# Modulation product in column strips, output pieces turned one per turn, half tiles of a V projection paired

## The chip, the cores and the metric

The kernel runs on one core of one Trainium2 chip. The metric is the device time of one execution, in microseconds; lower is better. TensorE (PE) multiplies, VectorE (DVE), ScalarE (ACT) and GpSimd (POOL) do the rest, and the sync engine (SP) issues most transfers.

## What is computed

Two blocks on 512 tokens of width 1024, all in float32. The first is an RWKV-7 time mixer with 16 heads of 64, whose recurrence is worked out in chunks of 64 tokens. The second is a block with a Fourier branch and a neighbourhood attention over the tokens and 256 context tokens; both inputs are normed and then modulated by a shift and a scale. The part of the reference that the change touches, cut to what matters (the bodies of the helpers are left out):

```
sh_x, sc_x, g_x = modulation of silu(c) @ w_ada + b_ada        # (1024) @ (1024, 3072)
sh_c, sc_c, g_c = the same for c_ctx
xn = rms_norm(x) * (1 + sc_x) + sh_x
cn = rms_norm(ctx) * (1 + sc_c) + sh_c
... vx ... = xn @ w_in        ... vc ... = cn @ w_in
y = (groupnorm(y) + bonus * v) * g                             # end of the RWKV mixer
out = y @ w_out
```

## The kernel before

One program of five instruction streams, one per engine, written out by hand and tied by semaphores; each engine works strictly in the order of its own stream. Weights come in 74 blocks through a ring of three buffers (`weights`, L469): SP may load block n when the engine that uses block n-3 is done with it.

The recurrence is a loop of 21 turns, g = -1 to 19 (L787 for PE, L1275 for ACT, L1631 for DVE). There are 16 groups of work (8 chunks by 2 halves of the heads). In turn g, PE starts group g+1 (`off_product` L656, `turned` L639, `grow` L668 and L670), goes on with group g (`rhs_values` L681, with `gram` L624 for group g+2) and finishes group g-1 (`from_state` L698 and L705, `scan_sa` L716, `scan_out` L729 and L737). Between them ACT and DVE take results out of PSUM: `mask_gram` L1564, `mask_z` L1572, `add_x` L1581, `update` L1595 and L1596 on DVE; `copy_sa` L1252, `copy_y` L1258 on ACT. At the end of some turns DVE also norms a finished quarter of y: `centre` (L1605 to L1607) where g % 4 is 1, a sum of squares (L1655) where it is 2, a scaling (L1658, L1659) where it is 3.

Two other pieces of work stand inside the turns. **Modulation**: silu(c) and silu(c_ctx), as two columns `SILC`, times `w_ada`, in 12 blocks of 256 output columns. `mods_here(g, k)` (L774) puts a block into slot k of turn g by the table `MODS_BY` (L457): slot 0 lies between `turned` and `grow`, slot 1 between `rhs_values` and `gram`. A slot is `turn_mods` (L755, two small transposes of the block before, copied to `MROW` by ACT, L1264) and `modulation` (L741, eight products through `accumulate` L513, with the two columns stationary and 128x256 weights moving). Before, turns 0 to 5 carry two blocks each, and turn 6 the last `turn_mods`. DVE then makes shift and scale of them (`take_mods`, L1618) at the end of turn 7. **Turning**: in turns 8, 12 and 16, PE turns a quarter of y in four pieces of four transposes (`turn_y`, L759, L771): pieces 0 and 2 from y, 1 and 3 from the bonus values. All use bank 3, the bank of the modulation too, and so each waits until the piece before is taken: 0 and 2 by ACT (`take_y`, L1271), 1 and 3 by DVE (`finish_y`, L1614, L1616).

Later, in the second block, `vv` (L905) is the V projection: for two halves of 256 columns, seven tiles of 128 tokens (five of the padded tokens `XNP`, two of the context) each in eight products of `accumulate`, two tiles to a bank. `XNP` is 64 zero columns, 512 tokens and 64 zero columns wide, so the first half of tile 0 and the last half of tile 4 are zeros. ACT takes the banks (`take_v`, L1358). The K projection behind it (L507 to L509) uses weights that ACT and DVE split into two parts (L1118, L1706).

A product of plain float32 shows as two instructions in the trace; a transpose as one.

## Time and profile before

| what | value |
|---|---|
| median of 3 runs | 916.29 us (915.19 to 919.98) |
| the profiled execution | 915.69 us, of it 913.9 us span |
| mean granted clock | 0.942 |
| TensorE busy | 809.0 us, 89% |
| VectorE, ScalarE, GpSimd busy | 501.6, 301.0, 209.4 us |
| bytes moved | 72.82 MB, 80 GB/s |

The span runs from the first to the last instruction; the time of the execution holds 1.8 us more. A wait in square brackets at the end of a row is idle time of that engine just before the instruction, with the instruction that ended it. In the view by stretch a row has the stretch, its length, then busy time and number of instructions of PE, PE's weight loads, DVE, ACT and POOL, then granted clock, share of the DMA engines and GB/s. A granted clock of 1.00 is 2.4 GHz, of 0.50 is 1.2 GHz; a share between is a stretch that had both.

### The profile page before, as it was taken

To read this page: it belongs to the slowest core of one execution; us is meant where nothing else is said; L and a number is where in the kernel's file an instruction comes from. 1 tells how busy PE (TensorE), PEld (TensorE's weight loads), DVE (VectorE), ACT (ScalarE), POOL (GpSimd) and SP (SyncE) were. 2 spreads that over 40 slices of the span, in tenths; PEclk is the share of its full clock that TensorE was granted. 3 is DMA by queue.
4 is the path that set the end of the run, shared out by engine and by line. 5 is a ranking of instruction groups with operands and counts; after the bars stand their busy time and mean duration, and the time that the engine had idled before them with its cause. 6 is when DMAs were issued, how large, how long until landed. Compare 5 with 4: busy or idle time off the path is not lost.

```text
span 913.9 us, 17380 instructions
## 1 busy us (share of the span) xinstructions
PE 809.0 (89%) x7476; PEld 642.2 (70%) x7476; DVE 501.6 (55%) x799; ACT 301.0 (33%) x625; POOL 209.4 (23%) x162
## 2 busy tenths in 40 slices
PE   2599998999796899987877899999979988989997
PEld 2288775777585566676876788888756766767597
DVE  4973998988676212165544212802995646543711
ACT  6334433455331112132323135512334433322410
POOL 0254422445343011132211000630000000000662
PEclk9799999999798799998988999999998998989999
DMA  7023241323437544410003033401320211121221
GB/s 219 23 74 108 73 136 48 93 70 82 103 116 185 117 140 140 141 48 3 4 3 139 30 109 91 87 24 47 93 69 24 59 37 45 47 81 47 93 82 58
DMA packets 116621, 72.82 MB, mean 80 GB/s; under 512 B 26816, under 2 KB 113984, under 8 KB 116544
## 3 DMA queue, kind: packets, MB, share of 16 engines
q1 hardware_dynamic: 81856, 64.07, 23.3%
q10 hardware_dynamic: 34688, 7.62, 4.1%
q8 instruction: 60, 0.98, 0.4%
q14 instruction: 17, 0.14, 0.0%
HBM read 64.35 MB, written 7.34 MB: 78 GB/s over the span
## 4 chain that ended last, share of the span: by engine, by line
PE 76%; DVE 13%; ACT 3%; issue 2%; DMA 2%; ACTq 1%; POOL 1%; POOLq 0%; DVEq 0%
PE bank L513 24%; PE bank L932 8%; PE bank L507 5%; PE bank L508 5%; PE bank L509 5%; DVE arena L1466 3%; PE bank L954 2%; PE bank L967 2%; PE bank L624 2%; DVE arena L1564 2%; PE bank L670 2%; PE bank L656 2%; PE bank L1050 1%; PE bank L1052 1%; PE bank L1051 1%
## 5 line engine op out<-in xcount | busy, mean ns | idle before, releaser
L513 PE MATMUL bank<-arena 128*128 128x256 f32 (+2 forms) x1024 | 242.3, 396 | 4.5 <-DVE arena L1616 3.1
L513 PEld LDWEIGHTS bank<-arena 128*128 128x128 f32 (+1 forms) x1024 | 175.9, 175 | 62.9 <-issue 17.3
L1869 POOL TENSOR_TENSOR w_lo<-arena,w_hi 128x1024 fp32r<-128x1024 f32 x24 | 62.6, 2610 | 110.6 <-ACT w_hi L1118 110.6
L507 PE MATMUL bank<-x_hi,w_hi 128*128 128x512 f32 x192 | 80.5, 419 | 4.9 <-DVE x_lo L1472 4.9
L1118 ACT ACTIVATE w_hi<-arena 128x1024 fp32r<-128x1024 f32 x44 | 46.5, 1057 | 93.6 <-DMA arena<-w_in 92.3
L509 PE MATMUL bank<-x_hi,w_lo 128*128 128x512 f32 x192 | 77.1, 402 | 0.0
L508 PE MATMUL bank<-x_lo,w_hi 128*128 128x512 f32 x192 | 77.0, 401 | 0.0
L1971 POOL COPY arena<-arena 128x512 f32<-128x512 f32 x4 | 2.5, 614 | 223.8 <-DVE arena L1789 223.8
L507 PEld LDWEIGHTS bank<-x_hi,w_hi 128*128 128x128 f32 x192 | 37.1, 193 | 15.8 <-issue 7.7
L1564 DVE TENSOR_TENSOR arena<-bank,arena 128x512 f32<-128x512 f32 x32 | 20.6, 686 | 49.0 <-PE bank L624 49.0
L1706 DVE TENSOR_TENSOR w_lo<-arena,w_hi 128x1024 fp32r<-128x1024 f32 x20 | 25.0, 1250 | 38.3 <-ACT w_hi L1118 38.3
L1908 POOL TENSOR_TENSOR arena<-arena 128x512 f32<-128x512 f32 x16 | 20.1, 1258 | 110.0 <-PE bank L716 106.7
L1768 DVE TENSOR_REDUCE arena<-bank 128x1 f32<-128x256 f32 x32 | 13.6, 424 | 56.4 <-PE bank L947 56.4
L508 PEld LDWEIGHTS bank<-x_lo,w_hi 128*128 128x128 f32 x192 | 37.2, 194 | 9.9 <-issue 1.7
L509 PEld LDWEIGHTS bank<-x_hi,w_lo 128*128 128x128 f32 x192 | 37.1, 193 | 8.7
L932 PE MATMUL bank<-xn_hi,w_hi 128*128 128x512 f32 x96 | 41.3, 430 | 0.0
L1466 DVE SCALAR_TENSOR_TENSOR arena<-arena 128x512 f32<-128x512 f32 x48 | 40.6, 916 | 0.0
L1581 DVE TENSOR_TENSOR arena<-arena,bank 128x128 f32<-128x128 f32 x48 | 12.0, 285 | 51.5 <-PE bank L670 51.4
L932 PE MATMUL bank<-xn_lo,w_hi 128*128 128x512 f32 x96 | 39.1, 407 | 0.0
L932 PE MATMUL bank<-xn_hi,w_lo 128*128 128x512 f32 x96 | 38.8, 404 | 0.0
L1404 ACT ACTIVATE arena<-arena 128x256 f32<-128x256 f32 x32 | 16.3, 509 | 62.2 <-DVE arena L1772 61.6
L1050 PE MATMUL bank<-w_out_hi,mix_hi 128*128 128x256 f32 x128 | 36.5, 286 | 0.2 <-DVE mix_lo L1836 0.2
(237 smaller groups left out, 1691.9 us busy)
## 6 DMA issues: line engine op xcount, KB each, us to landing
arena<-w_in SPq DMA_DIRECT2D x45, 512.0 KB, 4.0
arena<-w_ada SPq DMA_DIRECT2D x12, 1024.0 KB, 5.2
arena<-w_in SPq DMA_DIRECT2D x8, 1024.0 KB, 5.6
arena<-w_out SPq DMA_DIRECT2D x8, 1024.0 KB, 5.1
lt_dram<-arena ACTq DMA_DIRECT2D x16, 256.0 KB, 2.3
arena<-x SPq DMA_DIRECT2D x4, 512.0 KB, 7.3
arena<-x SPq DMA_DIRECT2D x1, 2048.0 KB, 7.7
out<-arena SPq DMA_DIRECT2D x8, 256.0 KB, 2.6
```

The costliest lines, as they stand in the source:

```text
L507: mm(o[:, :], w_hi[:, wk], x_hi, start=(k == 0), stop=False)
L508: mm(o[:, :], w_hi[:, wk], x_lo, start=False, stop=False)
L509: return mm(o[:, :], w_lo[:, wk], x_hi, start=False, stop=(k == KT - 1))
L513: last = mm(o, lhs(k), rhs(k), start=(k == 0), stop=(k == n - 1))
L932: last = mm(banks[5 + i % 2][:, :], w[slot][:, k * P:(k + 1) * P], v[k][:, :], start=(r == 0), stop=(r == 3 * KT - 1))
L1050: mm(oi, MXHI[k][:, at], W2HI[nb][:, wk], start=(k == 4), stop=False)
L1118: A(WHI[n % 3][:, :], WR[n % 3][:, 0:1024], ACT.Copy).then_inc(weights_rounded, 1)
L1466: ins = STT(MIXES[m][:, c, :], DX[:, c, :], vec("mu_" + "wakrvg"[m], c), HT[:, c, 1:T + 1], MUL, ADD)
L1564: free(TT(GM[g % 4][:, h], o, gram_mask.unsqueeze(1).broadcast_to([P, 4, 2 * CH]), MUL), ("gram", g, h))
L1706: TT(WLO[n % 3][:, :], WR[n % 3][:, 0:1024], WHI[n % 3][:, :].bitcast(f32), SUB)\
L1869: TT(WLO[n % 3][:, :], WR[n % 3][:, 0:1024], WHI[n % 3][:, :].bitcast(f32), SUB)\
L1908: TT(XS[:, g % 3].rearrange("p s c (m n) -> p (s c) m n", n=BLK), x.unsqueeze(2).broadcast_to([P, 8, CH // BLK, BLK]), blocks.broadcast_to ...
```

## The change

Modulation: `SILC` is now 32 columns wide (two and thirty zeros, cleared by DVE). The eight products of a block go to four strips of 32 columns of the array, two products summed in each, and leave four partial sums in PSUM partitions 0, 32, 64 and 96. ACT copies all 128 partitions, and `turn_mods` is now two plain products with a constant `pick` (128x2, ones where the partition modulo 32 is the column), which turn and add the four in one. The last four blocks move to slot 1 of turns 4 to 7, the last `turn_mods` to turn 8 (slot 0), `take_mods` to the end of turn 8.

Turning: quarters 0 and 1 of y are turned one piece a turn, in turns 8 to 15; ACT takes its piece in the even turns, DVE in the odd ones. Quarter 2 still goes in one turn, 16.

V projection: tiles are taken in the order 1, 2, 3, 5, 6, 0. The last stands for tiles 0 and 4: their halves with tokens go side by side to two strips of 64 columns. The zero halves of V are cleared by GpSimd instead.

```diff
-               ("reset", T), ("dft128", 2 * P), ("eps", 3)]:
+               ("reset", T), ("dft128", 2 * P), ("eps", 3), ("pick", 2)]:
...
+    put("pick", (i % 32 == j[:, 0:2]).astype(f))
...
-        MROW = fixed.take(256, 2)
+        SILC = fixed.take(KT * 32).rearrange("p (c k) -> p c k", k=32)
...
+        MROW = arena[:, ht_at + 1536:ht_at + 1792]
...
+        V_TILES = (1, 2, 3, 5, 6, 0)
...
-        for n, (g, k) in enumerate([(0, 0), (0, 1), (1, 0), (1, 1), (2, 0), (2, 1), (3, 0), (3, 1), (4, 0), (4, 1), (5, 0), (5, 1),
-                                    (6, 1)]):
+        for n, (g, k) in enumerate([(0, 0), (0, 1), (1, 0), (1, 1), (2, 0), (2, 1), (3, 0), (3, 1), (4, 1), (5, 1), (6, 1), (7, 1),
+                                    (8, 0)]):
...
-                last = accumulate(banks[MODS_BANK][0:2, 0:256], lambda k: SILC[:, k, :], lambda k: w[:, k, :])
+                for r in range(2):
+                    for q in range(4):
+                        k = 2 * q + r
+                        last = mm(banks[MODS_BANK][32 * q:32 * q + 32, 0:256], SILC[:, k, :], w[:, k, :], start=(r == 0),
+                                  stop=(r == 1), skip_group_check=True)
...
-                    last = nc.tensor.transpose(banks[MODS_BANK][:, at:at + 2], MROW[:, h * P:(h + 1) * P], ident[0:2, 0:2])
+                    last = mm(banks[MODS_BANK][:, at:at + 2], MROW[:, h * P:(h + 1) * P], con("pick"), start=True, stop=True,
+                              skip_group_check=True)
...
-                if turning:
+                if 8 <= g < 16:
+                    turn_y(g // 4 - 2, g % 4)
+                if g == 16:
                     for piece in range(4):
-                        turn_y(g // 4 - 2, piece)
+                        turn_y(2, piece)
...
+                    for i, t in enumerate(V_TILES[2 * b3:2 * b3 + 2]):
+                        oi = o[:, i * 256:(i + 1) * 256]
+                        if t:
...
+                        for k in range(KT):
+                            for h, at in ((0, 4 * P), (1, HD)):
+                                last = mm(oi[side[h], :], XNP[:, k, at:at + HD], w[:, k, :], start=(k == 0),
+                                          stop=(k == KT - 1), skip_group_check=True)
...
-                    A(MROW, banks[MODS_BANK][0:2, 0:256], ACT.Copy).then_inc(mods_copied, 1)
+                    A(MROW, banks[MODS_BANK][:, 0:256], ACT.Copy).then_inc(mods_copied, 1)
...
-                if turning:
-                    take_y(g // 4 - 2, 0)
-                    take_y(g // 4 - 2, 1)
+                if 8 <= g < 16 and g % 2 == 0:
+                    take_y(g // 4 - 2, g % 4 // 2)
...
-                if turning:
-                    finish_y(g // 4 - 2, 0)
-                    finish_y(g // 4 - 2, 1)
+                if g == 8:
+                    take_mods()
+                if 8 <= g < 16 and g % 2 == 1:
+                    finish_y(g // 4 - 2, g % 4 // 2)
...
-                if g == 7:
-                    take_mods()
...
+            own.did(nc.gpsimd.memset(VP[:, 0:5:4, :], 0.0))
```

PE, a turn that lost its slot 0 and kept slot 1 (turn 4), from `off_product` of turn 4 on. The rows give line, operation, tiles, size and number. Before:

```order
L656 MATMUL bank<-arena 64x32 x16
L639 MATMUL bank<-arena 64x64 x16
L755 MATMUL bank<-arena 128x2 x2
L513 MATMUL bank<-arena 2x256 x8
L668 MATMUL bank<-arena 64x32
```

and now, where L658, L641, L670 stand for the old L656, L639, L668:

```order
L658 MATMUL bank<-arena 64x32 x16
L641 MATMUL bank<-arena 64x64 x16
L670 MATMUL bank<-arena 64x32
L672 MATMUL bank<-arena 64x32
L670 MATMUL bank<-arena 64x32
```

The table took slot 0 out of the turn: `grow` follows `turned` at once.

PE, end of turn 8 and start of turn 9. Before:

```order
L729 MATMUL bank<-arena 64x64 x8
L737 MATMUL bank<-arena 64x64 x8
L771 MATMUL bank<-arena 128x2x64 x16
L656 MATMUL bank<-arena 64x32 x16
L698 MATMUL bank<-arena 64x64 x8
```

and now:

```order
L731 MATMUL bank<-arena 64x64 x8
L739 MATMUL bank<-arena 64x64 x8
L778 MATMUL bank<-arena 128x2x64 x4
L658 MATMUL bank<-arena 64x32 x16
L700 MATMUL bank<-arena 64x64 x8
```

One piece of four transposes is left in the turn; the same four rows end each of turns 8 to 15.

DVE, from the end of turn 13 to the first `mask_z` of turn 14. Before:

```order
L1595 TENSOR_TENSOR arena<-bank,arena 128x256
L1596 TENSOR_TENSOR arena<-arena 128x256
L1605 TENSOR_REDUCE arena<-arena 128x16
L1606 TENSOR_SCALAR arena<-arena 128x16
L1607 TENSOR_TENSOR arena<-arena 128x1024
L1572 TENSOR_TENSOR arena<-bank,arena 128x8x16
```

and now:

```order
L1616 TENSOR_TENSOR arena<-bank,arena 128x256
L1617 TENSOR_TENSOR arena<-arena 128x256
L1635 TENSOR_TENSOR arena<-arena,bank 128x512
L1637 SCALAR_TENSOR_TENSOR arena<-arena 128x512
L1626 TENSOR_REDUCE arena<-arena 128x16
L1627 TENSOR_SCALAR arena<-arena 128x16
L1628 TENSOR_TENSOR arena<-arena 128x1024
L1593 TENSOR_TENSOR arena<-bank,arena 128x8x16
```

The two instructions of `finish_y` now stand ahead of `centre` and of the `mask_z` that PE waits for. The same pair stands at the end of turns 9, 11 and 15.

## Rows read from the trace of the kernel before

**Rows 1.** The page, part 1: busy time, share of the span and instructions of each engine.
```profile
PE 809.0 (89%) x7476; PEld 642.2 (70%) x7476; DVE 501.6 (55%) x799; ACT 301.0 (33%) x625; POOL 209.4 (23%) x162
```

**Rows 2.** The page, part 4: shares of the chain that ended last, by engine.
```profile
PE 76%; DVE 13%; ACT 3%; issue 2%; DMA 2%; ACTq 1%; POOL 1%; POOLq 0%; DVEq 0%
```

**Rows 3.** Busy time by stretch: turn 5, then turns 8 to 13 of the recurrence.
```profile
374.90:389.75 14.85, 14.33 (x277) 9.35 (x277) 2.96 (x9) 2.93 (x8) 2.04 (x3) 1.00 0.44 143
...
407.97:422.23 14.26, 9.67 (x256) 8.25 (x256) 7.27 (x18) 5.18 (x14) 2.44 (x4) 0.90 0.01 2
422.23:430.88 8.65, 8.15 (x242) 7.87 (x241) 4.17 (x10) 2.18 (x6) 1.66 (x2) 0.76 0.02 4
430.88:441.04 10.16, 8.27 (x241) 7.69 (x241) 6.29 (x13) 3.01 (x7) 3.78 (x4) 0.83 0.02 4
441.04:447.96 6.92, 6.42 (x240) 6.14 (x241) 4.46 (x11) 2.35 (x7) 2.54 (x4) 1.00 0.02 5
447.96:461.76 13.80, 9.75 (x258) 8.34 (x260) 6.81 (x15) 5.19 (x14) 2.45 (x4) 0.95 0.01 2
461.76:471.01 9.25, 8.75 (x240) 8.47 (x241) 4.19 (x10) 2.18 (x6) 1.66 (x2) 0.70 0.01 4
```

**Rows 4.** TensorE in order of time, slot 0 of turn 1; then one form's busy us, mean ns.
```profile
318.60 0.28 PE L755 MATMUL bank<-arena 2*128 2x2 f32 x2
318.81 3.61 PE L513 MATMUL bank<-arena 128*2 128x256 f32 x16
322.35 0.31 PE L668 MATMUL bank<-arena 64*64 64x32 f32 x4
322.49 0.29 PE L670 MATMUL bank<-arena 64*64 64x32 f32 x4
...
L513 PE MATMUL bank<-arena 128*2 128x256 f32 x192 | 44.9, 388 | 0.0
```

**Rows 5.** TensorE in order of time: products in half tiles; then L967's durations, ns min/median/max.
```profile
358.12 1.10 PE L624 MATMUL bank<-arena 64*64 64x128 f32 x32
...
747.07 1.09 PE L967 MATMUL bank<-arena 128*64 128x128 f32 x16
...
L967 PE MATMUL bank<-arena x256: 272/273/476, 703.5 to 830.3; 128*64 128x128 f32 x128
```

**Rows 6.** TensorE in order of time: pieces 0, 1 and 3 turned in turn 8.
```profile
415.18 0.66 PE L771 MATMUL bank<-arena 128*128 128x128 f32 x4
417.43 0.65 PE L771 MATMUL bank<-arena 128*128 128x128 f32 x4 [1.59 <-ACT arena L1271]
...
421.19 1.11 PE L771 MATMUL bank<-arena 128*128 128x128 f32 x4 [1.59 <-ACT arena L1271]
```

**Rows 7.** VectorE in order of time, end of turn 8.
```profile
415.86 0.60 DVE L1596 TENSOR_TENSOR arena<-arena 128x256 f32<-128x256 f32 x1
418.19 0.69 DVE L1614 TENSOR_TENSOR arena<-arena,bank 128x512 f32<-128x512 f32 x1 [1.74 <-PE bank L771]
418.92 0.69 DVE L1616 SCALAR_TENSOR_TENSOR arena<-arena 128x512 f32<-128x512 f32 x1
```

**Rows 8.** TensorE in order of time: the wait for `mask_z` in turns 8 and 10.
```profile
410.89 0.31 PE L668 MATMUL bank<-arena 64*64 64x32 f32 x4 [0.55 <-DVE arena L1572]
...
434.89 0.31 PE L668 MATMUL bank<-arena 64*64 64x32 f32 x4 [1.64 <-DVE arena L1572]
```

**Rows 9.** TensorE in order of time: second V projection, what follows it.
```profile
578.70 48.51 PE L513 MATMUL bank<-arena 128*128 128x256 f32 x224
626.86 0.58 PE L507 MATMUL bank<-xn_hi,w_hi 128*128 128x512 f32 x1
```

**Rows 10.** VectorE and GpSimd in order of time, around the second V projection.
```profile
591.98 1.87 DVE L1706 TENSOR_TENSOR w_lo<-arena,w_hi 128x1024 fp32r<-128x1024 f32 x1
...
562.17 0.85 POOL L1947 MEMSET arena<- 128x256 f32 x1
```

**Rows 11.** The page, part 6: a transfer of modulation weights.
```profile
arena<-w_ada SPq DMA_DIRECT2D x12, 1024.0 KB, 5.2
```

More of the change, by code:

```diff
@@ L182, in rwkv_then_grid_block @@
         GST = small(64 * 3)
-        SILC = small(16).rearrange("p (c k) -> p c k", k=2)
         SILT = small(32)
@@ L788, in _ @@
                 now, nxt, old = 0 <= g < GROUPS, g + 1 < GROUPS, 0 < g <= GROUPS
-                turning = g in (8, 12, 16)
                 if nxt:
@@ L906, in _ @@
                 w = weights()
-                for b4 in range(4):
-                    o = next_bank(("vv", nb, b4))
-                    for i in range(2):
-                        t = 2 * b4 + i
-                        if t < 7:
-                            last = accumulate(o[:, i * 256:(i + 1) * 256],
-                                              (lambda k: XNP[:, k, t * P:(t + 1) * P]) if t < 5 else
-                                              (lambda k: CNT[:, k, (t - 5) * P:(t - 4) * P]), lambda k: w[:, k, :])
-                    full(last, ("vv", nb, b4))
+                for b3 in range(3):
+                    o = next_bank(("vv", nb, b3))
+                    for i, t in enumerate(V_TILES[2 * b3:2 * b3 + 2]):
+                        oi = o[:, i * 256:(i + 1) * 256]
+                        if t:
+                            last = accumulate(oi, (lambda k: XNP[:, k, t * P:(t + 1) * P]) if t < 5 else
+                                              (lambda k: CNT[:, k, (t - 5) * P:(t - 4) * P]), lambda k: w[:, k, :])
+                            continue
+                        for k in range(KT):
+                            for h, at in ((0, 4 * P), (1, HD)):
+                                last = mm(oi[side[h], :], XNP[:, k, at:at + HD], w[:, k, :], start=(k == 0),
+                                          stop=(k == KT - 1), skip_group_check=True)
+                    full(last, ("vv", nb, b3))
             for name in ("kk", "q"):
@@ L981, in _ @@
             for nb in range(2):
-                for b4 in range(4):
-                    stored(pe, ("vv", nb, b4))
+                for b3 in range(3):
+                    stored(pe, ("vv", nb, b3))
             for p in range(PU + 2):
@@ L1276, in _ @@
                 nxt, old = g + 1 < GROUPS, 0 < g <= GROUPS
-                turning = g in (8, 12, 16)
                 if old:
@@ L1290, in _ @@
                     fetch_inverse(1)
-                if turning:
-                    take_y(g // 4 - 2, 0)
-                    take_y(g // 4 - 2, 1)
+                if 8 <= g < 16 and g % 2 == 0:
+                    take_y(g // 4 - 2, g % 4 // 2)
+                if g == 16:
+                    take_y(2, 0)
+                    take_y(2, 1)
                 j = g // 4 - 1
@@ L1354, in take_v @@
                 for nb in range(2):
-                    for b4 in range(4):
-                        o = arrived(act, ("vv", nb, b4)).rearrange("p (i n) -> p i n", i=2)
-                        w = 2 if b4 < 3 else 1
-                        free(A(VP[:, 2 * b4:2 * b4 + w, nb * 256:(nb + 1) * 256], o[:, 0:w, :], ACT.Copy), ("vv", nb, b4))
+                    at = slice(nb * 256, (nb + 1) * 256)
+                    for b3 in range(3):
+                        o = arrived(act, ("vv", nb, b3)).rearrange("p (i n) -> p i n", i=2)
+                        if b3 < 2:
+                            t = V_TILES[2 * b3]
+                            ins = A(VP[:, t:V_TILES[2 * b3 + 1] + 1:b3 + 1, at], o, ACT.Copy)
+                        else:
+                            A(VP[:, 6, at], o[:, 0, :], ACT.Copy)
+                            for h, t in ((0, 4), (1, 0)):
+                                ins = A(VP[side[h], t, at], o[side[h], 1, :], ACT.Copy)
+                        free(ins, ("vv", nb, b3))
             def round_xn():
@@ L1445, in _ @@
             own.did(nc.vector.memset(CST, 0.0))
+            own.did(nc.vector.memset(SILC, 0.0))
             own.did(nc.vector.memset(HT[:, :, 0:1], 0.0))
@@ L1456, in _ @@
             own.own(TS(SILT[:, 16:32], SILT[:, 0:16], 0.5, 0.5, MUL, ADD))
-            own.did(TT(SILC.rearrange("p c k -> p k c"), SILT[:, 16:32].rearrange("p (k c) -> p k c", k=2),
+            own.did(TT(SILC[:, :, 0:2].rearrange("p c k -> p k c"), SILT[:, 16:32].rearrange("p (k c) -> p k c", k=2),
                        VECS[:, VEC["c"]:VEC["c"] + 16].rearrange("p (k c) -> p k c", k=2), MUL))
@@ L1632, in _ @@
                 now, nxt, old = 0 <= g < GROUPS, g + 1 < GROUPS, 0 < g <= GROUPS
-                turning = g in (8, 12, 16)
                 if nxt:
@@ L1646, in _ @@
                     update(g - 1)
-                if turning:
-                    finish_y(g // 4 - 2, 0)
-                    finish_y(g // 4 - 2, 1)
+                if g == 8:
+                    take_mods()
+                if 8 <= g < 16 and g % 2 == 1:
+                    finish_y(g // 4 - 2, g % 4 // 2)
+                if g == 16:
+                    finish_y(2, 0)
+                    finish_y(2, 1)
                 j = g // 4 - 1
```

## Prediction

> **What bounds the kernel now.** I read the page first. TensorE is busy 89% of the span [rows 1], and 76% of the chain that ended last is its work [rows 2]. So instructions taken off TensorE shorten the kernel, unless something else then ends the same turn. The busy time by stretch shows this for the recurrence, one row per turn [rows 3]. A turn without extras takes 6.92 us, of it 6.42 busy (turn 11). A turn with two modulation slots takes 14.85 (turn 5). A turn that turns four pieces takes 14.26 or 13.80 (turns 8 and 12), with 9.7 busy: the rest is waiting. The turns behind these, 9 and 13, take 8.65 and 9.25 at a clock of 0.76 and 0.70, so the waits cost a second time. Turn 10 follows `centre` and takes 10.16, at 0.83.
>
> **The modulation blocks.** In a slot the 16 instructions start every 0.215 us (3.61 less the last one's own 0.38, over 15), and from the block's start to `grow` it is 3.54 us [rows 4]. Each is 256 columns wide, so 0.215 us is the price of 256 columns on the full array, whether 2 or 128 stationary columns are used. What do strips give? Nothing in the trace has four strips. The nearest rows are products in halves [rows 5]. L967, two strips of 64 columns under all 128 rows, does 16 instructions of 128 columns in 1.09 us, one alone 0.27: 0.82 over the seven steps between eight pairs, about 0.11 to 0.12 a pair. That is about the full-array price of one (0.215 / 2), so two strips run fully side by side. L624 has four quarter tiles: 32 instructions of 128 columns in 1.10 us, seven steps in 0.83 after the first four, so four run side by side. Those are the two bounds: four strips fourfold, 16 x 0.215 / 4 = 0.86 us a block, or only twofold, 1.72. I add 0.10 for the change of shape, the 3.54 less 16 x 0.215. I take fourfold, since L624 is the row with four tiles. 12 x (3.54 - 0.96) = **31.0 us off**, all on the path, as no slot is preceded by a wait. The Trainium skill, TensorE: Matmul & The Clock Gate, section on packing small matmuls, gives a measured 2.38x for three column strips. At that efficiency, an estimate from that page, a block takes 1.09 and the sum is 2.7 us worse; the trace shows two strips at no loss, and no run here four.
>
> `turn_mods` becomes two float32 products, four instructions with 128 stationary columns each. Before, the next block starts 0.21 us after it starts [rows 4]. Four transposes with 128 stationary columns take 0.66 [rows 6], one alone 0.27 as in rows 5, so 0.13 a step. At 0.11 (half of 0.215) to 0.13 each that is about 0.44 a time: 12 x 0.23 = **2.8 us back**.
>
> Moving two slots out of turns 4 and 5 and into 6 and 7 changes no count. The weights stay ahead: one block's transfer takes 5.2 us [rows 11], three are in flight, and a turn of two blocks will take some 10 us. Even one after the other, block 7 lands about 30 us into the loop and is needed at about 36. Cost nothing; if that cover went, 1 or 2 us.
>
> **The turning.** In turn 8, PE waits 1.59 us before pieces 1 and 3 until ACT has taken the one before [rows 6], and less before piece 2. With one piece a turn these go. A single piece (0.5 to 0.6) mostly lies in the 0.50 that PE idles in each plain turn (6.92 less 6.42 [rows 3]), which is the wait for `mask_gram` at its start, so I cost it at 0.1 while that cover is there, 0.55 in turns 14 and 15, where there is no such wait. But two things are added.
> - In turn 8 the first piece needs bank 3, which `take_mods` frees. `take_mods` now stands behind `update`, which ends at 416.46 [rows 7], while PE's piece was ready at 415.18 [rows 6]. With `turn_mods` 0.4 later and 0.2 for the read, PE waits some 1.6 us. Against that the wait for `mask_z` in turn 8, 0.55 [rows 8], to which `take_mods` at the end of turn 7 belonged, goes. The next turn then starts near 417.2 instead of 422.23: **5.0 off**.
> - `finish_y` takes 1.42 us on DVE, from 418.19 to 419.61 [rows 7]. It now stands ahead of `centre` or the scaling in turns 9, 11, 13 and 15. Queued behind it are the `mask_z` that PE's `grow` waits for. Turn 10 already waits 1.64 there [rows 8]; it becomes 3.06. Turn 12 had none; it gets 1.4. Turn 14 is like turn 10.
>
> Turn by turn: turn 9 back to plain, 8.65 - 6.92 = 1.7 off. Turn 10, 1.4 on. Turn 12, 13.80 - 6.92 = 6.9 off, 1.4 on. Turn 13, 9.25 - 6.92 = 2.3 off. Turn 14, 1.9 on with its piece. Turns 15 and 16, 1.3 on (the piece, and some of `finish_y`, which now delays the third quarter). For the clock I add what turn 10 lost beyond its wait, 10.16 - 6.92 - 1.64 = 1.6, once more, because longer waits will let it fall again somewhere. With turn 8: -5.0 - 1.7 + 1.4 - 5.5 - 2.3 + 1.9 + 1.3 + 1.6 = **8.3 off**.
>
> **The V projection.** 224 instructions in 48.5 us, 0.215 each, and the K projection follows without a wait [rows 9]. Per half, 32 of 112 instructions (tiles 0 and 4) become 32 of half width. By L967 a pair of them costs what one full instruction costs: 16 x 0.215 = 3.44 instead of 6.88. Twice 3.44 = **6.9 us off**. The cover of what runs beside it holds: the split weights for the K projection are done at 593.85 [rows 10], the new end is near 620. GpSimd's added clearing is 1,024 wide, four times its 256-wide one of 0.85 [rows 10]: 3.4 us behind 563.0 at most, with the V projection starting at 578.70: nothing. The wider `SILC` clearing and ACT's extra copies lie under waits for transfers.
>
> **The sum.** 31.0 - 2.8 + 8.3 + 6.9 = 43.4 us. Against the profiled execution, 915.7, that is **872.3 us**. This execution lies 0.6 us below the median of 916.3; I leave that alone.
>
> **The rivals.**
> - Strips overlap only twofold. The two instructions of one product share a strip; if the engine starts matmuls strictly in program order, the second holds back the next strip, and only neighbours overlap. For it: no row has four strips. Against: L668 and L670 alternate in the program, yet run four and four [rows 4], and L624 runs four tiles at once [rows 5]. Price: 12 x 0.86 = 10.3 us, so 882.6. The Trainium skill, same page and section, says that matmuls are "strict FIFO, no reordering"; by that rule, this would be the outcome.
> - DVE becomes the bound of the late turns. If turns 10, 12 and 14 each lose the 1.6 us of clock on top of their longer waits, and turn 8 also, three more of them add 4.8; with pieces not hidden under the 0.50, eight times 0.5 more: 881. For it: turn 10's clock fell after 1.64 us of waiting [rows 3, 8]. Against: only DVE's order, not its load, is tight, 4.46 of 6.92 in turn 11.
> - Slower than before: four strips of 32 columns don't overlap, and each instruction waits for the one before to end, 0.38 instead of 0.215 [rows 4]. Place: the 12 blocks. A block then takes 6.06 + 0.10 us, 12 x 2.62 = 31.4 on. With the other terms, 12.4 off, that is 915.7 + 31.4 - 12.4 = 934.7. It decides from 4.6 us a block. Against it: halves do overlap [rows 5], and strips of 32 are a finer cut of the same thing. If they run one after the other without a gap, a block costs what it did and the time is 903.
>
> **Chances.** Forecast (872) 0.68; twofold 0.16; DVE and clock 0.09; no overlap, no gap 0.03; slower 0.03; something else, still faster, 0.01. The range for 8 in 10 must hold the forecast with its own spread, from -7 (no clock falls after the waits, and the wait at bank 3 is hidden) to +6, and the two rivals near 882: **865 to 885**. A measurement of this kernel tells about 0.5%, 4.6 us, from no change. Faster by more than that 0.96, within it 0.01, slower 0.03.
>
> **What would show it.** Blocks of 32-column products of about 0.95 us, or 1.8 (twofold), or over 4.6. Turns 1 to 3 of 9.4 to 10.2 us. No wait of 1.59 for ACT in turns 8 to 15, one of about 1.6 for DVE at bank 3 in turn 8, and waits for `mask_z` of about 3 us in turns 10 and 14, 1.4 in turn 12. The V projection at 41.6 us with no wait behind it. The prediction is wrong if a block lasts over 1.3 us, or if the turns from 8 to 15 are not some 8 us shorter in all.

## The result, and the profile after

The change takes the kernel from 916.22 us (median of 4 runs, 915.19 to 919.98) to 889.80 us (median of 4 runs: 892.07, 887.52, 896.19, 887.32). The ratio is 0.9708, 95% interval 0.9665 to 0.975. So 26 us are gone where the prediction had 43, and the time lies outside the predicted range of 865 to 885. The order of the four times is the order of their mean granted clocks: 0.934 twice (887), 0.925 (892), 0.920 (896); runs of before, taken beside the experiments below, spread as widely, from 914 us at 0.942 to 923 at 0.932. The profiled execution is the one of 892.07 us, with a span of 890.3, so one of the two slower.

The page, part 1, of the changed kernel, for [rows 1]:

```profile
PE 787.9 (89%) x7500; PEld 636.6 (72%) x7500; DVE 502.8 (56%) x800; ACT 301.5 (34%) x627; POOL 210.4 (24%) x163
```

TensorE is busy for 21.1 us less than before, and its share is the same 89%. Part 4, for [rows 2], where "issue", time in which an engine waited for nothing visible, has gone from 2% to 3%:

```profile
PE 76%; DVE 14%; issue 3%; ACT 3%; DMA 2%; ACTq 1%; POOL 1%; POOLq 0%; DVEq 0%
```

**The strips themselves did what was forecast.** TensorE in order of time, turn 2, for [rows 4]: start and length in us, line, form, count.

```profile
336.92 0.61 PE L761 MATMUL bank<-arena 128*128 128x2 f32 x4
337.45 1.07 PE L751 MATMUL bank<-arena 128*32 128x256 f32 x16
338.45 1.10 PE L626 MATMUL bank<-arena 64*64 64x128 f32 x32
```

From the block's start to the next work it is 1.00 us (337.45 to 338.45), forecast 0.96, where it was 3.54. In the trace the sixteen start in four groups of four, 0.007 us apart within a group and 0.22 to 0.24 us from group to group. `turn_mods` takes 0.53 (336.92 to 337.45), forecast 0.44. The V projection, for [rows 9]:

```profile
561.62 17.43 PE L515 MATMUL bank<-arena 128*128 128x256 f32 x80
578.98 3.67 PE L925 MATMUL bank<-arena 128*64 128x256 f32 x32
...
603.65 0.50 PE L509 MATMUL bank<-xn_hi,w_hi 128*128 128x512 f32 x1
```

It lasts 42.03 us, 6.1 less than before, and nothing waits behind it.

**The turns did not follow.** Busy time by stretch, one row a turn, turns 0 to 15 (5, 7, 9, 11 and 13 left out; they take 9.35, 9.43, 7.83, 7.54 and 6.99): the stretch, its length, busy us of PE, PEld, DVE, ACT, POOL, then the granted clock, the DMA share and GB/s.

```profile
300.05:314.29 14.24, 12.64 (x196) 9.48 (x197) 2.65 (x7) 1.70 (x5) 0.00 (x0) 0.50 0.56 144
314.29:330.60 16.31, 16.31 (x249) 13.04 (x249) 2.64 (x7) 2.57 (x7) 1.25 (x1) 0.50 0.43 137
330.60:341.15 10.55, 10.04 (x282) 8.42 (x281) 3.30 (x9) 2.95 (x8) 2.45 (x4) 0.98 0.52 158
341.15:352.43 11.28, 9.90 (x281) 8.29 (x281) 4.20 (x11) 3.23 (x9) 2.44 (x4) 1.00 0.68 216
352.43:361.28 8.85, 7.73 (x229) 6.70 (x229) 2.88 (x8) 2.18 (x6) 1.66 (x2) 1.00 0.29 87
...
370.63:384.26 13.63, 11.48 (x260) 9.65 (x261) 6.36 (x13) 3.94 (x9) 4.00 (x4) 0.75 0.28 94
...
393.69:404.87 11.18, 9.52 (x249) 8.72 (x249) 5.80 (x16) 2.18 (x6) 2.70 (x4) 0.85 0.17 61
...
412.70:425.00 12.30, 8.82 (x245) 8.27 (x244) 8.20 (x15) 3.02 (x7) 4.00 (x4) 0.86 0.02 3
...
432.54:441.11 8.57, 7.25 (x246) 6.70 (x245) 6.05 (x14) 2.19 (x6) 2.06 (x3) 1.00 0.02 4
...
448.10:461.11 13.01, 9.15 (x214) 8.54 (x213) 7.16 (x14) 3.02 (x7) 2.76 (x4) 0.74 0.01 3
461.11:469.46 8.35, 6.42 (x182) 5.57 (x182) 4.71 (x8) 4.26 (x12) 0.58 (x1) 1.00 0.01 2
```

Look at the clock of the first two rows, and then at the same two turns of before:

```profile
300.89:317.05 16.16, 14.56 (x194) 8.34 (x195) 2.62 (x7) 1.67 (x5) 0.00 (x0) 0.82 0.44 104
317.05:331.13 14.08, 13.57 (x244) 8.58 (x245) 2.87 (x8) 2.55 (x7) 1.66 (x2) 1.00 0.48 154
```

The forecast had 9.4 us less in turns 0 and 1, and they take the same time: 30.5 us for 30.2. The clock comes down to its lower level (0.50, 1.2 GHz) in the wait ahead of the recurrence in both kernels. Before, it was back at the upper one (1.00, 2.4 GHz) at 306.9:

```profile
289.80:306.90 17.10, 12.56 (x208) 9.43 (x201) 3.94 (x9) 1.32 (x4) 5.29 (x7) 0.50 0.50 70
306.90:331.10 24.20, 22.12 (x367) 13.28 (x365) 4.88 (x13) 3.56 (x10) 1.66 (x2) 1.00 0.47 148
```

Now it is not back before 331.0:

```profile
290.00:331.00 41.00, 35.51 (x581) 28.34 (x574) 8.93 (x22) 4.93 (x14) 6.79 (x9) 0.50 0.51 131
```

The other large item is the waits in the late turns. TensorE's waits from turn 0 on, by line and what ended them: us in total, times, longest.

```profile
PE bank L670 <- DVE arena L1593: 9.9, 4, 3.5
PE bank L658 <- DVE arena L1585: 5.8, 7, 1.6
...
PE bank L672 <- issue: 1.7, 3, 0.8
PE bank L658 <- issue: 1.4, 1, 1.4
PE bank L778 <- DVE arena L1643: 1.2, 1, 1.2
PE bank L718 <- issue: 1.2, 2, 0.6
```

The first row is `mask_z` at 3.48 in turns 10 and 14, 1.63 in turn 6 and 1.32 in turn 12, for [rows 8]. The three rows with "issue" make 4.3 us, with 0.5 of L670 4.8, in seven waits; before there was one, of 0.59, in turn 7.

Set against the prediction's own terms, by groups of turns (us, profiled executions):

| turns | before | forecast | after | missed by |
|---|---|---|---|---|
| 0, 1 (four blocks) | 30.2 | 20.9 | 30.5 | 9.6 |
| 2 to 5 (eight blocks, now six) | 58.6 | 37.0 | 40.0 | 3.0 |
| 6, 7 (none, now two) | 18.2 | 20.8 | 23.1 | 2.3 |
| 8 to 15 (the turning) | 79.6 | 71.7 | 75.8 | 4.1 |
| V projection | 48.2 | 41.3 | 42.0 | 0.7 |

The last column makes 19.7 of the 19.8 us between 872.3 and 892.07.

### The profile page after: what moved, and what is told of

Same layout as the page of the kernel before. It is cut to its first block, busy times and chain, and to the rows that moved or that the text cites. A ratio compares the mean times of both kernels' runs of the same rounds, so it can differ in the third digit from the quotient of the medians.

```text
span 890.3 us, 17431 instructions
## 1 busy us (share of the span) xinstructions
PE 787.9 (89%) x7500; PEld 636.6 (72%) x7500; DVE 502.8 (56%) x800; ACT 301.5 (34%) x627; POOL 210.4 (24%) x163
## 3 DMA queue, kind: packets, MB, share of 16 engines
q1 hardware_dynamic: 81856, 64.07, 23.9%
## 4 chain that ended last, share of the span: by engine, by line
PE 76%; DVE 14%; issue 3%; ACT 3%; DMA 2%; ACTq 1%; POOL 1%; POOLq 0%; DVEq 0%
PE bank L515 18%; PE bank L944 8%; PE bank L509 5%; PE bank L510 5%; PE bank L511 5%; DVE arena L1487 3%; PE bank L626 2%; PE bank L966 2%; PE bank L672 2%; PE bank L979 2%; PE bank L751 2%; PE bank L658 2%; DVE arena L1585 2%; PE bank L1062 1%; PE bank L1064 1%
## 5 line engine op out<-in xcount | busy, mean ns | idle before, releaser
L515 PE MATMUL bank<-arena 128*128 128x256 f32 (+1 forms) x768 | 184.3, 399 | 4.6 <-DVE arena L1637 3.1
L515 PEld LDWEIGHTS bank<-arena 128*128 128x128 f32 x768 | 148.2, 196 | 38.4 <-issue 15.4
L1424 ACT ACTIVATE arena<-arena 128x256 f32<-128x256 f32 x32 | 16.3, 510 | 61.8 <-DVE arena L1794 61.2
L1064 PE MATMUL bank<-w_out_hi,mix_lo 128*128 128x256 f32 x128 | 36.0, 282 | 0.0
```

The costliest lines, as they stand in the source:

```text
L515: last = mm(o, lhs(k), rhs(k), start=(k == 0), stop=(k == n - 1))
L1064: last = mm(oi, MXLO[k][:, at], W2HI[nb][:, wk], start=False, stop=(k == 3))
```

## The experiments

The theories. CLOCK: the dense blocks at the start had raised the clock, and the strips do the same work without raising it. WORK, its rival: the strips are worth less on the path than their own length says, whatever the clock. For the late turns, FINISH: the two instructions of `finish_y` ahead of the next `mask_z` are paid in full. All times are medians; each ratio is to the kernel before, run beside it (916 us each time).

**1. The old form of the blocks, the rest as changed (e1_full_blocks).**

```
-  for r in range(2): for q in range(4): last = mm(bank[32q:32q+32, 0:256], SILC[:, k, :], w[:, k, :], ...)
+  last = accumulate(bank[0:2, 0:256], lambda k: SILC[:, k, 0:2], lambda k: w[:, k, :])
```

(with the old copy of two rows and the old transposes).

> The changed kernel with the twelve modulation blocks and their turning back in the old form (two stationary columns, full array), all else as changed. The changed kernel took 889.8 us where 872.3 was forecast. Theory CLOCK: the strips are as fast as forecast, but TensorE's granted clock stays at 0.50 through turns 0 and 1 (290 to 331 us) because the dense blocks that raised it at 307 us are gone. Then here turns 1 and 2 run at 1.00 again, turn 1 takes about 14.1 us instead of 16.3, and the strips turn out to be worth only some 18 us: about 908 us. Rival WORK: the low clock there has nothing to do with the strips; it stays low here too until 331, and the kernel takes the full 28 us more, 918.

Measured: 906.73 us (904.5 to 908.79), ratio 0.989 (0.9857 to 0.9923). Its clock, to the end of turn 1:

```profile
289.70:306.70 17.00, 13.14 (x210) 9.59 (x202) 3.94 (x9) 1.32 (x4) 5.31 (x7) 0.50 0.50 73
306.70:330.66 23.96, 21.85 (x366) 13.19 (x365) 4.91 (x13) 3.56 (x10) 1.65 (x2) 1.00 0.47 149
```

Nothing but the dense blocks was put back, and the early rise is there again. The time is near CLOCK's 908 and not at WORK's 918. By the medians the strips are worth 16.9 us (906.73 less 889.80), not the 28.2 of the sum (31.0 less 2.8).

**2. Dense work ahead of turn 0 (e2_warm).** Seven products of 512 columns without a use, four behind the last g product and three behind `gram(0)`:

```
+            for _ in range(4):     # and range(3) behind gram(0)
+                mm(banks[6][:, :], ident, con("reset"), start=True, stop=True)
```

> The changed kernel with seven dense products of constants (128x128 by 128x512, into a bank nobody reads) put where TensorE only waits before the recurrence: four behind the last g product, three behind the first gram. Their result is used by nobody. Theory CLOCK: the clock no longer falls at 290 us, turns -1, 0 and 1 run at 1.00: about 2.5 us less in turn -1, 3 in turn 0, 7 in turn 1, together 10 to 12 us off: 879 us. If strips cannot hold the clock up by themselves, it falls again within turn 0 or 1 and only 3 to 5 us are won: 885. Rival WORK (clock not decisive there): no gain, 890, or 1 to 3 us slower by the added products.

Measured: 887.27 us (886.59 to 891.41), ratio 0.9688. The clock stayed up until 299.60, and then:

```profile
291.79:299.60 7.81, 6.22 (x184) 4.84 (x186) 2.70 (x8) 0.66 (x2) 5.22 (x7) 1.00 0.41 64
299.60:326.90 27.30, 25.70 (x378) 19.59 (x373) 4.71 (x12) 4.16 (x12) 1.25 (x1) 0.50 0.58 154
```

The 2.5 us by which the median is lower are within the noise (the intervals of the two ratios overlap); the trace is what counts here. It is not only that the recurrence begins at the lower level. In turns 0 and 1 with strips the clock falls by itself, though TensorE is busy for 25.70 of the 27.30 us.

**3. The turning as before (e3_no_spread).** All four pieces, with `take_y` and `finish_y`, at the end of turns 8 and 12 again; `take_mods` stays at the end of turn 8.

```
-                if 8 <= g < 16:
-                    turn_y(g // 4 - 2, g % 4)
+                if g in (8, 12, 16):
+                    for piece in range(4):
+                        turn_y(g // 4 - 2, piece)
```

> The changed kernel with the turning of y back in turns 8 and 12, four pieces in one turn; take_mods stays at the end of turn 8. The forecast for the spreading was 8.3 us off. If that holds, 898. The trace of the changed kernel shows for turns 8 to 15 waits of 3.5 us in turns 10 and 14 and clocks of 0.86 and 0.74; summed over turns 8 to 15 it took 75.8 us against 77.1 before, with one piece of turn_mods and the bank 3 wait in it. Theory DVE ORDER: the spreading is worth only 1 to 4 us, because finish_y now delays mask_z: 891 to 894. Rival: it is worth its 8, and the time was lost elsewhere.

Measured: 897.6 us (889.69 to 898.47), ratio 0.9763 (0.9707 to 0.9818). By the medians that is 7.8 us over the changed kernel, by the ratios 5.0, and the intervals overlap: whether the spreading gains anything is not settled by the time. Nor is this run the turning of before. With `take_mods` at the end of turn 8 its turn 8 takes longer than the 14.26 us of [rows 3], for TensorE waits 1.48 us for it at bank 3 and then for each piece:

```profile
389.21:406.03 16.82, 10.84 (x260) 9.16 (x260) 7.27 (x18) 5.20 (x14) 2.45 (x4) 0.89 0.12 42
```

Turns 8 to 14 take 78.2 us in this profile, 71.1 before and 67.4 in the changed kernel. So the run cannot confirm the 8.3 of the sum, which was reckoned from before. The 897.6 is the rival's 898, but the theory of VectorE's order isn't refuted by it: run 7 bears it out.

**4. The V projection as before (e4_no_pair).**

```
-  V_TILES pairs, tiles 4 and 0 as halves side by side in one piece of the bank
+  for b4 in range(4): for i in range(2): accumulate over whole tiles 0 to 6
```

> The changed kernel with the second V projection as before (seven full tiles, no pairing, no clearing of V by GpSimd). The trace shows 42.0 us for it where there were 48.2: 6 us slower, 896, if nothing behind it takes the gain back; 890 if something does.

Measured: 896.18 us (893.51 to 898.73), ratio 0.9775, 6.4 us over the change, forecast 6.9; the intervals of the two ratios just overlap. In its trace the projection is again 224 instructions, from 561.34 to 609.49 (48.15 us). This term held.

**5. One dense block (e7_dense_first).** Block 0, in slot 0 of turn 0, is one accumulation into rows 0 to 31; blocks 1 to 11 in strips.

```
+                if n < 1:
+                    last = accumulate(banks[MODS_BANK][0:32, 0:256], lambda k: SILC[:, k, :], lambda k: w[:, k, :])
```

> Against the change, only block 0 of the modulation product (turn 0) is put back into one dense accumulation of eight products (into rows 0 to 31 of the bank, the copy and the turning of that block over these rows); the other eleven stay in column strips. Theory CLOCK (the change lost what it had saved because in turns 0 and 1 the array was too little used for the clock to rise, 0.50 until 331.0 us where before it rose at 306.9): the dense block costs some 3 us more in turn 0 (5.1 for 1.9), the clock is up soon behind it, turn 1 lasts 10.4 to 11 us for 16.3 and the rest of turn 0 goes faster: 884 us, with one stretch at 0.50 that ends near 307. Rival RATE (it is not the first block but the dense work over both turns that raises the clock): the clock stays at 0.50 until about 331, turn 0 is 3 us longer: 893 us. Rival NOISE (the clock's phase decides, not the work): anything between, and no link to the first block.

Measured: 885.98 us (884.65 to 887.51), ratio 0.9662 (0.961 to 0.9714). Turns 0, 1 and 4:

```profile
299.81:314.09 14.28, 12.68 (x197) 8.50 (x197) 2.62 (x7) 1.69 (x5) 0.00 (x0) 0.77 0.50 116
314.09:323.74 9.65, 9.14 (x249) 7.52 (x249) 2.88 (x8) 2.57 (x7) 1.66 (x2) 1.00 0.71 225
345.67:357.62 11.95, 11.95 (x228) 10.10 (x229) 2.65 (x7) 2.18 (x6) 1.26 (x1) 0.57 0.29 91
```

The dense block takes 5.52 us in place of 1.93, most of it at the lower clock, and for that turn 1 takes 9.65 instead of 16.31: 6.6 us less for the two turns, as CLOCK has it. Half of it went again where the clock fell once more, in turn 4 (11.95 for 8.85). The time alone would not show it, as the interval of the ratio overlaps that of the changed kernel.

**6. One dense block and the seven products (e8_dense_warm).**

> Block 0 dense, and the seven dense products without a use ahead of turn 0 (four behind the last g product, three behind the first gram). With the seven alone the clock stayed up 6 us longer, fell in turn 0 at 299.6 and stayed at 0.50 for 27.3 us: 887.3 us. Theory CLOCK: with block 0 dense it falls for less than 17 us or not at all, turns 0 and 1 last some 13 and 10.5 us: 880 us. Rival RATE (block 0 is too short to hold or raise it): 888 us or more.

Measured: 883.74 us (877.18 to 886.46), ratio 0.9622. The clock fell twice, 3.4 us from 298.0 and 10.2 us from 311.7; turns 0 and 1 took 12.82 and 14.29. The median is 2.2 us below that of run 5 and 3.5 below that of run 2, both within the intervals. One dense block doesn't hold the clock.

**7. `finish_y` a turn later (e5_late_finish).** From the end of turns 9, 11, 13 and 15 on VectorE to behind `add_x` of the next turn, ahead of `mask_gram`:

```
                if now:
                    add_x(g, 1)
+               if 10 <= g <= 16 and g % 2 == 0:
+                   finish_y((g - 1) // 4 - 2, (g - 1) % 4 // 2)
...
-               if 8 <= g < 16 and g % 2 == 1:
-                   finish_y(g // 4 - 2, g % 4 // 2)
```

> The change with only the finish moved, as said for the run with both. Theory FINISH (TensorE waits 3.48 us in turn 10, 1.32 in turn 12 and 3.48 in turn 14 for mask_z because the finish of the turn before stands ahead of it on VectorE): each wait 1.4 us shorter, 885.5 us. Rival: the waits are set by what ends the turn before (the norm of the tile), and the move only shifts them: 889 to 890 us, or slower by 1 to 2 us if the finish now delays the gram mask and with it the expansion.

Measured: 877.71 us (872.43 to 880.65), ratio 0.956 (0.9504 to 0.9616). VectorE ahead of turn 10's `mask_z` (L1593) in the changed kernel:

```profile
413.32 0.67 DVE L1635 TENSOR_TENSOR arena<-arena,bank 128x512 f32<-128x512 f32 x1
414.02 1.68 DVE L1637 SCALAR_TENSOR_TENSOR arena<-arena 128x512 f32<-128x512 f32 x1
415.63 1.21 DVE L1626 TENSOR_REDUCE arena<-arena 128x16 f32<-128x1024 f32 x1
...
417.08 1.23 DVE L1628 TENSOR_TENSOR arena<-arena 128x1024 f32<-128x1024 f32 x1
418.22 0.48 DVE L1593 TENSOR_TENSOR arena<-bank,arena 128x128 f32<-128x128 f32 x2
```

L1635 and L1637 are `finish_y`: 2.31 us from 413.32 to 415.63, not the 1.42 of [rows 7], because the second takes 1.68 for 0.69. When it began, GpSimd was in an instruction of its own (the bonus values times v):

```profile
413.20 1.96 POOL L1953 TENSOR_TENSOR arena<-arena 128x1024 f32<-128x1024 f32 x1
```

This is so throughout. In the fourteen traces this second instruction of `finish_y` runs 112 times. It takes 1.50 to 2.16 us in 21 cases and 0.69 in 91, and the 21 are exactly those in which GpSimd was in an instruction when it began. Three times GpSimd began after it; it then took its 0.69, and GpSimd's instruction took 1.66 to 1.71 where it otherwise takes 1.27.

TensorE's wait behind it, first in the changed kernel, then in this run, with turns 10 and 14 of this run by stretch:

```profile
418.56 0.31 PE L670 MATMUL bank<-arena 64*64 64x32 f32 x4 [3.48 <-DVE arena L1593]
```

```profile
411.69 0.31 PE L670 MATMUL bank<-arena 64*64 64x32 f32 x4 [1.63 <-DVE arena L1593]
407.68:417.21 9.53, 7.32 (x246) 6.74 (x245) 8.35 (x15) 3.57 (x9) 4.41 (x5) 1.00 0.01 4
440.24:449.97 9.73, 7.72 (x214) 7.16 (x213) 6.51 (x14) 3.02 (x7) 2.73 (x3) 0.82 0.01 3
```

So 1.85 of the 3.48 was the finish, and 1.63 the centring. That it is 1.85 and not 2.31 is the same meeting again: now an instruction of `centre` stands beside that GpSimd instruction (here 408.18 to 410.14), and takes 0.63 for the 0.17 of the changed kernel, 0.46 more.

```profile
409.54 0.63 DVE L1627 TENSOR_SCALAR arena<-arena 128x16 f32<-128x16 f32 x1
```

Turns 10, 12 and 14 take 9.5, 7.7 and 9.7 us for 12.3, 8.6 and 13.0, turns 8 to 15 together 69.5 for 75.8: the waits by which they are shorter are 5.0 us, most of the rest is clock that didn't fall. FINISH holds, and is worth more than was expected. Of the 12.1 us between the medians some may be chance: in this profile the turns ahead of the edit also came out shorter (turns 0 and 1, 26.4 for 30.5, the clock being up for 6.8 us in between).

**8. Both edits (e9_dense_late).**

> Both edits together: block 0 dense, and in turns 9, 11, 13 and 15 VectorE's finish of a half of the turned output is moved into the next turn, behind add_x and ahead of the gram mask, where VectorE had idle time. Theory CLOCK with the finish as a cause of the waits for mask_z: 880 us, the two gains (5.5 and 4) added. Rival (the waits in turns 10 and 14 are set by the bank and by the norm, not by the finish): 884 us, the same as with the dense block alone. Rival (the dense block does nothing): 886 to 889.

Measured: 878.66 us (873.02 to 881.05), ratio 0.9568 (0.9514 to 0.9622). The same as the late finish alone (877.71), so the expected 880 is met without what it stood for: in this trace the clock rose at 306.3 and fell again from 316.5 to 326.8, so turn 1 took 14.30. One dense block raises the clock in time, but whether it stays up is open. The two gains did not add.

**9. The centring a turn later as well (e10_late_both).**

```
-  if g in (9, 13): centre(j)                     # at the end of the turn
+  if g in (6, 10, 14): centre(g // 4 - 1)        # behind add_x and the late finish_y
```

(turn 5's likewise; the square, the sum and the root follow a turn later).

> To the late finish (877.7 us, waits for mask_z of 1.63 us left in turns 6, 10 and 14) the centring of a finished tile is moved the same way on VectorE: from the end of turns 5, 9 and 13 into turns 6, 10 and 14, behind add_x and ahead of the gram mask; its square and root on ScalarE and its sum on VectorE follow a turn later. Theory PLACE (both pieces of VectorE work stood between the state update and the first mask_z of the next turn, and TensorE paid for each in full): the three waits go, 4.9 us, and some of the stretches at 0.50 around them: 872 us. Rival GAP (the centring is longer than the idle time in its new place and now delays the gram mask): the waits move to the next turn, 876 to 880 us.

Measured: 882.94 us (880.03 to 885.35), ratio 0.9601, by the medians 5 us above run 7, with overlapping intervals. The waits for `mask_z` are gone from turns 6, 10 and 14, and this is what came, in turns 10 to 15:

```profile
PE bank L658 <- DVE arena L1590: 3.8, 2, 3.2
PE bank L672 <- issue: 1.5, 2, 0.8
...
PE bank L672 <- DVE arena L1598: 1.2, 1, 1.2
```

L1590 is `mask_gram`, L1598 `mask_z`, now waited for in turn 15. Finish and centring together overran the gap, and TensorE waited 3.2 us at the end of turn 10. Turns 8 to 15 add up to 69.7 us, as with the late finish alone: rival GAP, though the time lies above its 876 to 880. What makes it worse in the profiles is mostly the clock of turns 0 and 1, at 0.50 for 41 us in this one (30.5 for 26.4 us), which the edit doesn't touch.

**10. Two dense blocks (e12_late_dense2).** The kernel of run 9 with blocks 0 and 1 dense, `if n < 2`.

> Both moved pieces, and blocks 0 and 1 (turn 0) as one dense accumulation each, the other ten in strips. Theory CLOCK: up near 307 and, unlike with block 0 alone, it stays up through turn 1 in all runs; turns 0 and 1 last some 26 us, against 26.4 to 30.5 in the kernels in strips: 868 to 872 us, and a narrower spread. Rival (the second dense block costs 1.6 us and buys nothing): 873 us, as the kernel with both moved pieces or slower.

Measured: 877.49 us (875.57 to 878.59), ratio 0.9536 (0.9482 to 0.959), 5.5 us less than run 9 by the medians, and the four runs now agree within 3 us.

```profile
290.20:307.30 17.10, 13.19 (x215) 10.32 (x206) 3.94 (x9) 1.31 (x4) 5.31 (x7) 0.50 0.49 69
307.30:416.50 109.20, 93.07 (x2702) 79.05 (x2700) 46.39 (x108) 32.81 (x84) 24.49 (x32) 1.00 0.37 119
```

The clock stays up for 109 us. The size was 5 us off the expected 868 to 872 (the overrun gap in turns 10 and 15 is still in it), the mechanism as expected.

**11. Half of the product left out (e11_half_blocks).** One product a strip, 4 a block for 8. Half of the contraction is not computed.

> The change, with half of the modulation product left out: one product a strip in place of two (the second half of the contraction is not computed), so that a block has 4 products for 8, some 0.5 us at full clock. 48 products fewer. Theory FLOOR (the strips' time is on TensorE's path): 6 us less at the same clock, 884 us. Theory CLOCK (less work in the array costs as much as it saves in turns 0 to 7): 888 to 892 us, with a first stretch at 0.50 of 41 us or more. For the waits that end on nothing visible (4.7 us in turns 4 to 11 of the change, each some 1.4 us behind a 16 KB packet of the instruction queue): theory SUPPLY (TensorE runs out of instructions) has them shrink below 2 us in turns 4, 5 and 7 where 16 to 32 instructions fewer are issued in a turn; rival (they hang on the packet's place and not on the rate) leaves them or makes them longer.

Measured: 882.39 us (2 runs, 880.0 and 884.77), ratio 0.9597 (0.9522 to 0.9672). In total 7.4 us less, near FLOOR's 884, and CLOCK in the form written down here falls: it had 888 to 892, and a first stretch at 0.50 of 41 us or more, which lasted 37.5 (289.6 to 327.1). Strips with half the work did not hold the clock down longer. But all of the gain is in turns 0 to 4 (53.6 us for 61.2). Turns 5 to 8 took 43.83 us with the half product and 43.59 with the whole one. Where it went, turns 5 to 8 of this run:

```profile
PE bank L641 <- issue: 7.7, 4, 2.1
PE bank L658 <- DVE arena L1584: 2.1, 4, 0.5
```

The waits for nothing visible got longer (2.09, 1.63, 2.14, 1.87), not shorter, so SUPPLY in the form that was written down falls: the number of instructions in a turn does not set them. A limit on their rate is not excluded, for these turns also use them up faster (1,005 in 33.35 us of busy time at a clock of 0.96, for 1,029 in 37.59 at 0.88).

**12. One piece to a gap (e13_one_piece).** The kernel of run 10, but only tile 0 centred late (turn 6, where no finish stands), tiles 1 and 2 at the end of turns 9 and 13 as in the change.

> The kernel with both moved pieces and two dense blocks (877.5 us), but with one piece of VectorE work at most in a gap: the finish moved in all turns, the centring only for tile 0 (into turn 6, where no finish stands); tiles 1 and 2 are centred at the end of turns 9 and 13 as before. Theory GAP (in turns 10 and 14 centring and finish together overran the gap, and TensorE paid with 3.2 us ahead of turn 11 and 1.2 more in turns 10 and 15): these waits go, the wait of 1.63 us for mask_z in turns 10 and 14 comes back, turn 6 keeps its 9.8 us: 875 us or a little less. Rival (only the sum of VectorE's work counts, wherever it stands): 877.5 us again. And a check on the clock: up near 307 in this run as in every run with a dense block 0, or the link is broken.

Measured: 875.99 us (6 runs, 874.88 to 881.28), ratio 0.9551 (0.9509 to 0.9593). The 3.2 us at the end of turn 10 are gone, the 1.63 are back, turn 6 takes 9.49. The clock is up from 306.7 to 381.8, once more at the same place.
The two slower of the six runs are 878 and 881, so the narrower spread of run 10 isn't confirmed. This kernel and that of run 10 can't be told apart in time. Either is faster than the changed kernel (0.9551 against 0.9708, intervals apart) and than the one before. Neither can be told from run 7 (877.71), which has no dense block: its profile had the early rise by chance. The late finish with two dense blocks and the centring left where it was, has not been run.

**All profiles side by side.** The clock in the first turns, over every kernel (us):

| kernel | dense blocks in turn 0 | stretches at 0.50 in turns 0, 1 | turns 0 + 1 | median |
|---|---|---|---|---|
| before | 2 | to 306.9 | 30.2 | 916.2 |
| 1, old form | 2 | to 306.7 | 30.6 | 906.7 |
| changed | none | to 331.0 | 30.5 | 889.8 |
| 4, V as before | none | to 330.9 | 30.5 | 896.2 |
| 9, late finish and centring | none | to 330.9 | 30.5 | 882.9 |
| 11, half the product | none | to 327.1 | 26.9 | 882.4 |
| 3, turning as before | none | to 306.6, 313.5 to 327.1 | 26.3 | 897.6 |
| 7, late finish | none | to 305.9, 312.7 to 326.4 | 26.4 | 877.7 |
| 2, seven products | none | 299.6 to 326.9 | 29.2 | 887.3 |
| 5, one dense | 1 | to 306.4 | 23.9 | 886.0 |
| 8, one dense, late finish | 1 | to 306.3, 316.5 to 326.8 | 28.3 | 878.7 |
| 6, one dense, seven products | 1 | 298.0 to 301.4, 311.7 to 321.9 | 27.1 | 883.7 |
| 10, two dense | 2 | to 307.3 | 26.3 | 877.5 |
| 12, two dense | 2 | to 306.7 | 26.4 | 876.0 |

Two dense blocks in turn 0: up by 307.3 and up through turn 1 in four profiles of four. None: never up through turn 1, in seven of seven, and with whole strips and nothing ahead of them these two turns take 26.3 us or 30.5, in kernels that are the same up to there. One: up through turn 1 in one of three. So the strips alone, when the clock happens to rise near 306, are as short as two dense blocks, and what these buy is that it rises there each time. Each line is one execution; the slower runs of before, 923 us at 0.932, were not profiled. The 20.9 us of the forecast was not reached by any (23.9 at best).

## Why the prediction was wrong, point by point

- **"12 x (3.54 - 0.96) = 31.0 us off, all on the path."** This is the step that failed. The 0.96 was right (1.00 measured), the rival of a twofold overlap is out, and so are both on the other side. Of the rule that matmuls are "strict FIFO, no reordering" (the Trainium skill, TensorE: Matmul & The Clock Gate, packing small matmuls) I had worked out a twofold overlap; the trace has the sixteen instructions in 1.00 us, four at a time, so what I derived from it does not hold here. What failed is the words "all on the path": they took the clock of each turn as given. In turns 0 and 1 it depended on the very work that the change thins out. The forecast had 9.4 us off there, the trace 0.3 us more. Runs 1, 5, 10 and 12 show the link, from the dense side each time. What it is in the strips that leaves the clock low is not shown; it isn't idle time, and run 11 says that it isn't simply less work either.
- The trace of before had the sign of it. Its clock rises at 306.9, in the middle of the very block that the change makes small (block 0, started at 303.65 and lasting 5.18 us for the 3.61 of [rows 4]); I read the clock only for the late turns, behind waits [rows 3], and not where it came up. Busy time would not have told: turn 1 of the changed kernel is busy for 16.31 of 16.31 us at 0.50.
- **`turn_mods`, 2.8 back.** 0.53 a time for 0.44: 1.1 us more over twelve. The pieces' step of 0.13 would have given 0.52, and the prediction took the other end of its own bounds, 4 x 0.11.
- **Turns 2 to 5, 3.0 us short.** About 2.0 of it is waits for nothing visible (1.38 at the end of turn 3, where 0.51 for `mask_gram` stood before, 0.61 in turn 4, 0.55 in turn 5), which the prediction had no term for; the rest is the blocks and `turn_mods`, 0.13 a time over.
- **Turns 6 and 7, 2.3 short.** Turn 6 ran at 0.75 of the clock: 6.9 us at 0.50, where before there were 3.4. The 0.61 of such a wait in turn 7 is no part of the miss, as before had 0.59 there. What let the clock fall in turn 6 wasn't isolated. In runs 10 and 12, without the wait of 1.63 us for `mask_z` in that turn, it stayed up; in run 9, without it as well, it fell there for 3.4 us.
- **The turning, 8.3 off.** The places were right: no wait of 1.59 for ScalarE in turns 8 to 15, 1.20 at bank 3 in turn 8 (forecast 1.6), 3.48 for `mask_z` in turns 10 and 14 (forecast 3.06), 1.32 in turn 12 (1.4). By the profiles the turns came out 3.8 us shorter, not 8. `finish_y` was mis-sized, 2.31 for 1.42 in turns 10 and 14: the 1.42 was read where GpSimd stood still, and the change moved the piece beside a GpSimd instruction. Waits for nothing visible add 1.1. The larger part is the clock again. The sum kept 3.2 us of it (turn 10's 1.6, and 1.6 once more); the changed kernel has 13.7 us at 0.50 in these turns, which cost up to half of that, 6.9. Turn 14 alone, at 0.74, took 13.01, where the same turn without the wait and at 1.00 took 6.66 (run 9) and the wait was 3.48. Run 7 takes the waits away and much of it goes. Rival "DVE and clock" (881) was this mechanism at too small a price and too small a chance.
- **The V projection, 6.9 off.** 6.1 by the traces, 6.4 by run 4. A pass of half tiles lasts 3.6 us for 3.44.

The single misses are one thing: of the 20 us, some 9.6 (turns 0 and 1), and most of 4.1 and 2.3, are TensorE at the lower clock; for the clock the sum had 1.6 us and the range 6 us upward for everything. Even the two faster runs, 887.3 us, lie outside the range.

What stays open: what makes strips leave the clock low, why one dense block holds it in one trace and not in two others, and what the waits for nothing visible are.

## What to carry to other kernels

When an edit thins out TensorE's work, look up where in the profile the granted clock rises and falls before you credit the time, and ask whether the work you remove is what stands there; a saving priced at the upper clock can be lost whole in the turns at the lower one. If it is, try the dense form for the first few units: here two of twelve blocks, which brought the clock up near 307 in both profiles with them, worth 5.5 us by the medians against the same kernel without them, though the kernel with the late finish alone is as fast. When work is moved within an engine's stream, look at what is queued behind it, whether the gap holds all that is put there (two pieces overran it by 3.2 us), and what the other engines do at that time: VectorE's price of an instruction, read where GpSimd stood still, was 0.69 us and became 1.68.

## What the runs showed that was not expected

- From the start of sixteen float32 instructions of 256 columns in four column strips to the next work it is 1.00 us at the upper clock and 1.86 at the lower. That is a little over a quarter of the 3.54 us that the same sixteen take on the full array.
- In the recurrence TensorE stops every so often for nothing that the profile shows. In the changed kernel seven such waits, of 0.30 to 1.38 us, stand 125, 252, 503, 252, 251 and 503 of its instructions apart, which is one, two or four times about 126; in run 11 four stand 252, 251 and 252 apart. In both, each ends 1.2 to 1.4 us behind the end of a packet of 16,384 bytes on the queue that brings instructions, the first one 1.8. The page counts them:

```profile
q8 instruction: 60, 0.98, 0.5%
```

Before there was one of 0.59 us, 1.35 behind such a packet. With faster turns they grew, up to 2.14 us, and in run 11 they gave back all that the halved product had saved in turns 5 to 8. The page has 7,500 matmuls and 7,500 weight loads of TensorE, 250 to each of the 60 packets; by this estimate a packet holds about 125 matmuls, the distance of the waits. That they are instructions coming late fits this and the packets; no run moved or removed a packet, so this is argued and not shown.
- A VectorE instruction of 128 x 512 takes 0.69 us, and 1.50 to 2.16 when GpSimd is in an instruction as it begins (21 of 21 against 0 of 91, run 7 above). The kernel of before never had this pair meet, so its rows could not price it.
